# One MoE decoder step: at six of 32 expert positions a 2 MB weight transfer goes out as four small ones and a rest

## The reference

```python
logits = x2d @ w_router + b_router
top_v, top_i = lax.top_k(logits, TOP_K);  gates = softmax(top_v)
# for the tokens xb that chose expert e:
h = xb @ w_gate_up[e] + b_gate_up[e]               # 1024 -> 2048
out = clamped_swiglu(h) @ w_down[e] + b_down[e]    # 1024 -> 1024
y = sum over a token's experts of gate * out
x = x + y
```

## Time and profile before

| what | us |
|---|---|
| median of 3 runs | 1117.62 |
| lowest, highest | 1107.11, 1118.29 |
| the profiled execution | 1116.12 |
| its span, first to last instruction | 1114.2 |

### The profile page before, as it was taken

One profiled execution on the slowest core, in us unless ns is written; L12 is line 12 of the kernel. 1 busy time (PEld: TensorE's weight loads), 2 busy tenths in 40 slices (PEclk: granted clock), 3 DMA queues, 4 the chain that ended last, 5 costly groups with the idle time before them and its releaser, 6 DMA issues.

```text
span 1114.2 us, 16669 instructions
## 1 busy us (share of the span) xinstructions
PE 1000.4 (90%) x6626; PEld 427.8 (38%) x6626; DVE 393.0 (35%) x895; ACT 207.8 (19%) x451; POOL 11.0 (1%) x10
## 2 busy tenths in 40 slices
PE   9998999999997999889997999889789879979977
PEld 6766775333332333332332333233233323323323
DVE  7976646231322232222322132223333323222222
ACT  6864433111111111110110011011111111101101
POOL 2000000000000000000000000000000000000000
PEclk9959999999998999989998999999999999989989
DMA  9413973999999999999999999999999999999996
GB/s 365 137 43 100 391 298 117 381 420 428 412 429 425 427 423 413 427 426 428 407 428 425 429 408 430 426 427 429 426 429 427 426 427 427 428 426 428 427 427 269
DMA packets 43228, 425.22 MB, mean 382 GB/s; under 512 B 11412, under 2 KB 14740, under 8 KB 16656
## 3 DMA queue, kind: packets, MB, share of 16 engines
q1 hardware_dynamic: 42720, 423.56, 91.0%
q10 hardware_dynamic: 432, 0.52, 0.1%
HBM read 419.86 MB, written 2.51 MB: 379 GB/s over the span
## 4 chain that ended last, share of the span: by engine, by line
PE 60%; DMA 27%; DVE 6%; issue 3%; ACT 2%; SPq 1%; POOLq 0%; DVEq 0%; ACTq 0%
PE banks L551 57%; DMA gu_ring<-w_gu_dram 26%; SPq L429 1%; PE banks L987 1%; DVE raw L2008 1%; DMA w_in<-w_in_dram 1%; PE banks L938 1%; PE banks L994 1%; DVE hl L2020 1%; DVE hT L2025 1%; PE banks L1064 1%; ACT raw_s L1472 0%; PE banks L1071 0%; ACT gath L1428 0%; DVE hl L2017 0%
## 5 line engine op out<-in xcount | busy, mean ns | idle before, releaser
L2054 DVE TENSOR_TENSOR xT<-xT,banks 128x576 f32<-128x576 f32 x128 | 91.2, 751 | 534.9 <-PE banks L551 534.9
L551 PE MATMUL banks<-gu_ring,xe 128*64 128x512 f32 x1152 | 266.3, 599 | 12.2 <-DMA gu_ring<-w_gu_dram 12.0
L551 PE MATMUL banks<-gu_ring,xe_s 128*32 128x512 f32 x1152 | 157.6, 644 | 45.5 <-DMA gu_ring<-w_gu_dram 24.3
L551 PEld LDWEIGHTS banks<-gu_ring,xe 128*64 128x64 f32 x1152 | 75.3, 136 | 165.2 <-issue 141.2
L551 PE MATMUL banks<-dn_ring,hT 128*64 128x512 f32 x576 | 129.3, 597 | 4.9 <-DVE hT L2025 4.9
L551 PEld LDWEIGHTS banks<-gu_ring,xe_s 128*32 128x32 f32 x1152 | 29.6, 113 | 136.1 <-issue 100.0
L551 PE MATMUL banks<-dn_ring,hT_s 128*32 128x256 f32 x1152 | 67.8, 381 | 3.2 <-ACT xe_s L1462 3.2
L551 PEld LDWEIGHTS banks<-dn_ring,hT 128*64 128x64 f32 x576 | 39.2, 137 | 79.4 <-issue 73.0
L1443 ACT ACTIVATE raw<-banks 128x512 f32<-128x512 f32 x18 | 10.7, 597 | 232.0 <-PE banks L551 232.0
L551 PE MATMUL banks<-x_tok,oh 96*64 96x512 f32 (+1 forms) x228 | 50.3, 578 | 0.4 <-DVE oh L1979 0.4
L551 PE MATMUL banks<-gT,ye 64*128 64x288 f32 x288 | 50.5, 474 | 0.0
(11 more groups left out here) (361 smaller groups left out, 872.2 us busy)
## 6 DMA issues: line engine op xcount, KB each, us to landing
gu_ring<-w_gu_dram SPq DMA_DIRECT2D x120, 2048.0 KB, 21.2
dn_ring<-w_dn_dram SPq DMA_DIRECT2D x63, 2048.0 KB, 19.2
gu_ring<-w_gu_dram SPq DMA_DIRECT2D x16, 1024.0 KB, 8.5
w_out<-w_out_dram SPq DMA_DIRECT2D x2, 2048.0 KB, 10.0
w_in<-w_in_dram SPq DMA_DIRECT2D x3, 1024.0 KB, 12.4
w_in<-w_in_dram SPq DMA_DIRECT2D x4, 512.0 KB, 8.3
w_glu<-w_glu_dram SPq DMA_DIRECT2D x1, 2048.0 KB, 9.0
dn_ring<-w_dn_dram SPq DMA_DIRECT2D x2, 1024.0 KB, 21.5
```

The costliest lines, as they stand in the source:

```text
L551: return nc.tensor.matmul(out, lhsT, rhs, start=start, stop=stop, **kw)
L2054: X.tensor_tensor(two, two, pair[(1, 3)[n % 2]].rearrange("p (h f) -> p h f", h=2)[:, :, 0:T], ALU.add).then_inc(S("acc_done"), 1)
```

## The change

In the two places that correspond to PE's loops, SP now has loops of four and of six positions in a turn, and at the first position of each turn (positions 2, 6, 10, 14, 18 and 24, all of kind "few", all with an even number) the second down slot, `dn_ring[1]`, is filled by five transfers in place of one. Partitions 0 to 15 are sent by four transfers of eight partitions and half of each partition's 16 KB run (64 KB each), counted on a new semaphore `dn_low`; then partitions 16 to 127 by one transfer of 112 partitions, counted on `dn_in[1]` as before. PE waits for `dn_low` beside `dn_in[1]` at step c = 2 of `down` at these six positions. Bytes, order of the slots and everything else stay as they were.

```diff
+LOW = 16
...
-        with sp.Fori(0, PAIRS - 2) as i:
-            x = [expert_at(k, i * 2 + (k + 2)) for k in range(2)]
-            dn(x[0], i * 2, 0)
-            gu(x[0], i * 2 + 1)
-            dn(x[1], i * 2 + 1, 1)
-            gu(x[1], i * 2 + 2)
+        def dn_split(x, p_before):
+            sp.wait_ge(S("dn_used"), p_before * 4 + 2)
+            load_dn(sp, x, 0, 0)
+            sp.wait_ge(S("dn_used"), p_before * 4 + 4)
+            src = a["w_dn"][bass.ds(x, 1), 2:4].rearrange("o c p k f -> (o c p k) f").rearrange("(p i) f -> p i f", i=4)
+            for r in range(0, LOW, 8):
+                for i in (slice(0, 2), slice(2, 4)):
+                    sp.dma_start(dn_ring[1][r:r + 8, i], src[r:r + 8, i]).then_inc(S("dn_low"), 16)
+            sp.dma_start(dn_ring[1][LOW:], src[LOW:]).then_inc(dn_in[1], 16)
+
+        def two_experts(p, split):
+            x = [expert_at(k, p + k) for k in range(2)]
+            (dn_split if split else dn)(x[0], p - 2, *(() if split else (0,)))
+            gu(x[0], p - 1)
+            dn(x[1], p - 1, 1)
+            gu(x[1], p)
+
+        with sp.Fori(0, ROUNDS) as i:
+            for k in range(0, len(BODY), 2):
+                two_experts(i * len(BODY) + (2 + k), k == 0)
+        with sp.Fori(0, LATER) as i:
+            for k in range(0, len(LATE), 2):
+                two_experts(i * len(LATE) + (FIRST_LATE + k), k == 0)
...
+                if c == 2 and low is not None:
+                    pe.wait_ge(S("dn_low"), low)
...
+                if kind == "few" and c == 2 and low is not None:
+                    pe.wait_ge(S("dn_low"), low)
...
                 expert(i * 4 + (2 + k), i * (WIDE[6] - WIDE[2]) + WIDE[2 + k], i * (SLIM[6] - SLIM[2]) + SLIM[2 + k],
-                       BODY[k], BODY[k - 1], BODY[(k + 1) % 4], k % 2, i * 2 + (k // 2 + 2))
+                       BODY[k], BODY[k - 1], BODY[(k + 1) % 4], k % 2, i * 2 + (k // 2 + 2),
+                       (i * (4 * LOW) + 4 * LOW) if k == 0 else None)
```

More of the change, by code:

```diff
@@ L298, in build @@
     wu_in, wq_in = [S(f"wu_in{c}") for c in range(CT)], [S(f"wq_in{c}") for c in range(3)]
-    S("tail_done"), S("dn_last")
+    S("tail_done"), S("dn_last"), S("dn_low")
     gu_in = [S(f"gu_in{k}") for k in range(GU_SLOTS)]
@@ L1014, in combine_last, with down @@
                 last.then_inc(S("comb_done"), 1)
-        def down(w, s, kind, after, s_after, j, fill):
+        def down(w, s, kind, after, s_after, j, fill, low=None):
             def wide_part(c):
@@ L1116, in gate_bias, with expert @@
                     last.then_inc(S("comb_done"), 1)
-        def expert(p, w, s, kind, before, after, j, fill):
+        def expert(p, w, s, kind, before, after, j, fill, low=None):
             w_before, s_before = w - (before != "few"), s - (before != "mid")
@@ L1158, in expert @@
                 residual(LAST_PARTS[2])
-            down(w, s, kind, after, s_after, j, fill)
+            down(w, s, kind, after, s_after, j, fill, low)
         first_gather()
@@ L1172, in _ @@
                 expert(i * 6 + p, i * (WIDE[p + 6] - WIDE[p]) + WIDE[p], i * (SLIM[p + 6] - SLIM[p]) + SLIM[p],
-                       KINDS[p], KINDS[p - 1], KINDS[p + 1], k % 2, i * 3 + (p // 2 + 1))
+                       KINDS[p], KINDS[p - 1], KINDS[p + 1], k % 2, i * 3 + (p // 2 + 1),
+                       (i * (4 * LOW) + 4 * LOW * (ROUNDS + 1)) if k == 0 else None)
         expert(NE - 2, N_WIDE, N_SLIM - 2, "few", "mid", "few", 0, PAIRS)
```

## The result

The changed kernel takes 1165.17 us (median of four runs, 1162.65 to 1168.04), the kernel before 1117.78 us beside it (1107.11 to 1118.29). The ratio is 1.0465, 95% interval 1.0404 to 1.0525: 47 us slower, where 15 was forecast and the range ended at 1150. The direction was right, the size was not.

What follows compares the result with a forecast made beforehand. PE was taken to bound the first loop, DMA everything from 697 us. Two late splits 8.6 us, four earlier 11.2, less 5 absorbed, made some 15 us: 1132 us from the runs' median, range 1113 to 1150.

Steps and rivals of the forecast that it cites:

- What bounds the kernel: In the expert part, PE sets the pace in the first loop, and DMA from 697 us on.
- 1.5 us to spare in a turn: First loop: a turn lasts 119.4 us and its 24 transfers take 117.9 us, leaving DMA 1.5 us.
- The edits at no cost: SP's extra issues and longer loops, and PE's new wait, are covered by queued work or pass at once: nothing added.
- The pieces: Four 64 KB transfers per split take 1.23 us each, 4.9 in all; engines carrying them end 4.3 us later.
- The rest of 112 partitions gives each seven: At each split, the 112-partition transfer gives each engine seven partitions instead of eight, if spread evenly: 0.61 us less.
- rival 2: At each split the 112-partition transfer also loses time, some 6 us a split in all: 1148 us; chance 0.15.
- The absorption: At the kernel's end engines aren't level; if the pieces fall to early engines, some 5 us are absorbed.
- the room: The 1.5 us that DMA was said to have spare in each turn of the first loop, taking back part of the delay.
- The signs I named: PE's gu_ring waits grow, also in the first loop; GB/s drops some 5 us after splits, share near 1; landings differ.

Runs made afterwards that it cites:

- e14: Changed kernel with the slot sent whole and SP waiting at the six positions until the first down transfer has landed: 1131.99 us, ratio 1.0174.
- e2: Changed kernel with its longer SP loops, but the slot sent by one transfer of 128 partitions and PE without its new wait: 1116.48 us, ratio 1.0038.
- e8: Changed kernel with the slot at the six positions sent as two half-run transfers of all 128 partitions: 1115.51 us, ratio 0.9993.
- e3: Changed kernel without the four pieces and PE's new wait, only the 112-partition transfer sent at all six positions: 1159.68 us, ratio 1.0408.
- e9: Changed kernel with the 112-partition transfer, without pieces, at position 24 alone and full transfers at the other five: 1121.44 us, ratio 1.0045.
- e6: Changed kernel with the 112-partition transfer, without pieces, at positions 18 and 24 only and full transfers at the other four: 1126.86 us, ratio 1.0090.
- e7: Changed kernel with the 112-partition transfer, without pieces, at positions 2, 6, 10 and 14 only: 1136.73 us, ratio 1.0199.
- e15: Changed kernel sending only the 112-partition transfer, with SP waiting at the six positions until the first down transfer has landed: 1142.69 us, ratio 1.0259.

## Why the prediction was wrong, step by step

**What bounds the kernel**: held. PE set the pace in the first loop with DMA close behind, and all of the loss is DMA's: PE's waits for gu_ring there went from none to 36.7 us. That DMA has 1.5 us to spare in a turn was not measured by itself; e14, reckoned with it, came out 2 us from its expected value.

**The edits at no cost** (loops, issues, PE's wait, 8 KB runs): held, by e2 and e8. Neither has the four issues of the pieces; in the changed kernel these take 1.73 us at position 24, and GB/s is still 401 or more from 890 to 898.

**The pieces**: held in size by themselves, not in the kernel. I took 1.23 us each from the copy into 32 partitions; alone they take 1.0 and in a level stream 4.1 for four. But the reason I gave, a rate by the number of partitions, is wrong: eight scattered ones are faster than eight neighbours, and 64 neighbours take twice as long as 64 scattered ones. And in the kernel the pieces added some 5 us to the rest (e3), not the 15 that my forecast gave to them alone. That forecast and result point the same way is thus partly luck: the loss came from the other transfer.

**The step that failed** is "The rest of 112 partitions gives each seven, if it is spread evenly: 0.61 us less". Spread evenly it may be, but 112 partitions are another cut than 128, and a full transfer's 4.9 us become 7.5 by itself: 2.6 more instead of 0.6 less. With that corrected, the working would have given 4.1 + 2.6 = 6.7 us a split, 6 x 6.7 - 4 x 1.5 = 34 us, less the 5 us absorbed: 1147 (1152 without that). That was rival 2, to which I gave 0.15. I had its sentence ("another cut than eight") but priced it as an afterthought, since no row showed such a transfer; it should have weighed at least as much as the pieces, which were an eighth of the bytes.

**The absorption** failed too, and with the other sign. I took 5 us off because the engines aren't level. Their being out of step is no cushion. It makes each slow transfer slow its neighbours: 45 us come from six rests, and with the engines levelled six cost 11. In place of the 5 us absorbed there is a surcharge of some 13 us (47 - 34). That is a balance of two: at 2.6 us each, less the room, six rests would cost 6 x 2.6 - 4 x 1.5 = 10 us, and they cost 45; at 4.1 us each the pieces would cost 25 and they added 5.

**The signs I named**: PE's waits for gu_ring did grow in both loops, GB/s does drop behind each split at a share of 1, but for 18 us at the last one instead of 5, and over the rest, as rival 2 had it. The rest lands late (29.7 us after its issue in the median, against 22.6 for the full down transfers); when the pieces land I didn't read.

What stays open: which engines collide where. The traces show their sum, not whose write waits. How far the rests leave the engines apart in the kernel shows only at its end: the mean engine is done 2.7 us before the last in the kernel before, 3.2 with one rest (e9), 2.6 with two (e6), 4.3 with four (e7) and 6.9 with six (e3). So one or two rests leave no mark there that can be told, and in between nothing was measured. Why the pieces are partly hidden stays open too.

## What to carry to other kernels

Keep a stream of large loads uniform: all 128 partitions each, or a subset that is spread evenly (every second), never a block of neighbours and a remainder; the remainder is the dearer part. Price the large transfer that is left over as carefully as the small ones that are cut off it. And where DMA is the bound, read GB/s, not the busy share; one odd transfer in a stream without gaps also slows those beside it.

## What the hardware showed that I had not expected

- 112 partitions (1792 KB) take 7.5 us, 128 partitions (2048 KB) take 4.9: fewer bytes, half as long again.
- The same 64 partitions' worth of bytes takes 2.6 us as every second partition and 5.0 as a block, and in the kernel that is 0 against 41 us for twelve such transfers.
- Six equal rests in one execution (e3) are slow for 8, 12, 16, 20, 18 and 22 us; with the engines levelled before each (e15) for 9 to 12.
- A rest costs 7.3 us with level engines and about 13 with engines 8 us apart, with no other engine of the core at work.
- An added wait that empties the queue six times made the kernel that sends the rest alone 17 us faster (1159.68 to 1142.69).
- At that, DMA engines count as busy throughout (share 1.00 to 1.02 at 227 to 232 GB/s).
